# Layer norm, its projection, the second norm and the router's logits as one stage by halves and token tiles, in a fused block on one Trainium2 core

## The reference

```
y = silu(layernorm(conv(...), ln_g, ln_b))
y = y @ w_out
x = x + g1 * y
h = rmsnorm(x, norm_ffn_g[i]) * (1 + sc2) + sh2
grp_logits = (xt @ w_rg + b_rg)          # 4 groups
exp_logits = (xt @ w_re + b_re)          # 32 experts, top 2 in one group
x = x + g2 * hier_moe(h, ...)            # 32 experts: silu(x@gate) * (x@up) @ down
mod = c_act @ ada_w[i] + ada_b[i]        # gives g1, sc2, sh2, g2 ...
```

## Time and profile before

| | us |
|---|---|
| median of 3 runs (2859.23 to 2864.74) | 2859.59 |
| the profiled execution | 2864.43 |
| its span in the trace | 2862.3 |
| stretch from the start of the layer norm to the first expert matmul | 294.6 to 521.5 |
| busy in the whole span: PE, DVE, ACT, POOL | 2546.8, 1608.8, 953.9, 533.8 |

### The profile page before, as it was taken

How to read it: one execution, slowest core, us unless ns; L and a number is a source line. 1 busy time by engine, 2 the same in 40 slices (tenths; PEclk the granted TensorE clock), 3 DMA queues, 4 the chain that set the end, 5 groups by cost and what they waited for, 6 DMA issues and landing times. The chain is left out here.

```text
span 2862.3 us, 40467 instructions
## 1 busy us (share of the span) xinstructions
PE 2546.8 (89%) x15839; PEld 1397.2 (49%) x15839; DVE 1608.8 (56%) x2909; ACT 953.9 (33%) x1486; POOL 533.8 (19%) x476
## 2 busy tenths in 40 slices
PE   4999594799889998589799979998999999999978
PEld 3566343455445554245334447743554554645533
DVE  5876784322222222576499986543665656646742
ACT  6110503121112222555453225522443524514510
POOL 1011123000000000331341100000330411502413
PEclk8999796899999999799899989999999999999999
DMA  9553868599999998320102200043002002020052
GB/s 238 196 168 127 308 221 320 182 375 379 378 377 346 376 368 317 100 70 18 45 30 93 99 30 1 1 155 125 8 1 96 8 9 88 8 89 8 1 210 84
DMA packets 185104, 433.07 MB, mean 151 GB/s; under 512 B 26417, under 2 KB 35889, under 8 KB 184817
## 3 DMA queue, kind: packets, MB, share of 16 engines
q1 hardware_dynamic: 158112, 365.39, 35.8%
q0 software_dynamic: 10176, 32.78, 3.7%
q10 hardware_dynamic: 16656, 32.66, 3.3%
HBM read 371.85 MB, written 58.93 MB: 151 GB/s over the span
## 5 line engine op out<-in xcount | busy, mean ns | idle before, releaser
L1245 PE MATMUL m_gu<-conv_y,m_xT 128*64 128x256 f32 x1024 | 230.9, 384 | 20.2 <-DMA arena<-in_moe_w_up 17.9
L1323 DVE TENSOR_TENSOR m_hid<-m_sg,m_gu 64x256 f32<-64x256 f32 x96 | 39.6, 413 | 341.6 <-ACT m_sg L1293 341.6
L1247 PE MATMUL m_gu<-arena,m_xT 128*64 128x256 f32 x1024 | 230.9, 384 | 0.0
L2291 POOL TENSOR_TENSOR group_words<-steps,consts 128x1024 f32<-128x1024 f32 x32 | 66.0, 2067 | 684.1 <-PE i_pj L142 668.4
L1247 PEld LDWEIGHTS m_gu<-arena,m_xT 128*64 128x64 f32 x1024 | 141.9, 139 | 73.0 <-issue 15.4
L1267 PE MATMUL m_y_ps<-arena,m_hidT 128*64 128x512 f32 x768 | 175.4, 598 | 0.0
L140 PE MATMUL i_pj<-hT,group_words 128*128 128x512 f16 x384 | 146.5, 382 | 15.3 <-DVE group_words L410 9.4
L1245 PEld LDWEIGHTS m_gu<-conv_y,m_xT 128*64 128x64 f32 x1024 | 141.9, 139 | 36.8 <-issue 25.2
L1293 ACT ACT_TABLE_LOAD x48 | 61.6, 1283 | 286.4 <-issue 273.9
L140 PE MATMUL s_pj<-hT,arena 128*128 128x512 f16 x384 | 148.8, 387 | 0.0
L141 PE MATMUL s_pj<-hT,arena 128*128 128x512 f16 x384 | 148.5, 387 | 0.0
(11 more groups left out here) (519 smaller groups left out, 6386.3 us busy)
## 6 DMA issues: line engine op xcount, KB each, us to landing
arena<-in_moe_w_down SPq DMA_DIRECT2D x32, 2048.0 KB, 21.9
arena<-in_moe_w_up SPq DMA_DIRECT2D x22, 2048.0 KB, 24.9
conv_y<-in_moe_w_gate SPq DMA_DIRECT2D x22, 2048.0 KB, 20.8
hT<-in_moe_w_gate SPq DMA_DIRECT2D x10, 2048.0 KB, 21.6
hT<-in_moe_w_up SPq DMA_DIRECT2D x10, 2048.0 KB, 23.2
conv_y<-in_ada_w SPq DMA_DIRECT2D x8, 2048.0 KB, 8.0
x_tok<-in_ada_w ACTq DMA_DIRECT2D x6, 2048.0 KB, 12.7
slot_out<-m_y ACTq DMA_DIRECT2D x96, 128.0 KB, 6.2
```

The source lines that it names most:

```text
L1245: g = nc.tensor.matmul(gu_ps[i][g_rows, 0:FFN // 2], lhsT=xT[:, c, :], rhs=k.wg[e % WEIGHT_SLOTS][:, c, cols], start=c == 0, stop=c == KC - 1)
L1247: u = nc.tensor.matmul(gu_ps[i][u_rows, 0:FFN // 2], lhsT=xT[:, c, :], rhs=k.wu[e % WEIGHT_SLOTS][:, c, cols], start=c == 0, stop=c == KC - 1)
L1323: nc.vector.tensor_tensor(hid[:, i, :], sg[:, i, :], gu_ps[i][u_rows, 0:FFN // 2], ALU.mult) \
L2291: return k.nc.gpsimd.tensor_tensor(k.y_A[:, t % 2], k.adt[:, t, heads].unsqueeze(2).to_broadcast([P, HPG, P]), k.const("after").unsqueeze( ...
```

## The change

The four stages up to the logits become one, `front_stage`. The layer norm goes by halves: the products of token tiles 0 to 2 take channel chunks as the first half comes, and the second half is normalised beside them. The modulation sums stand ahead of the variance on PE, the eight late pieces behind token tiles 3 to 6 on DVE. Each token tile is then gated, added, squared, rooted, normalised, stored (from ACT's queue instead of SP's), transposed and multiplied for its logits. The norm's scale (1 + sc2) is folded into the router's weights, its shift into the router's bias, so `hT` holds the normed tokens without them. PSUM of the mean is reused as the third accumulator and for the transposes. The loads of expert weights stand at other places of SP's list.

```diff
+def front_stage(k):
...
+        ws = arena_units(k, 4, 2).bitcast(F16).rearrange("p (a c n) -> p a c n", a=2, c=KC)
+        normed = arena_units(k, 3).rearrange("p (t d) -> p t d", t=4)
+        ring = [arena_units(k, n).rearrange("p (c n) -> p c n", c=KC) for n in (2, 1)]
+        sums, gate = sb("sums", [P, 4, HALF]), sb("gate", [P, D])
+        rstd, mean1 = sums[:, 0:2], sums[:, 2]
...
+        acc_of, held = [0, 1, 2, 0, 1, 0, 1, 0], {3: 0, 4: 1, 5: 3, 6: 4, 7: 5}
+        turns_behind = {4: (0, 1), 5: (2, 3), 6: (4,), 7: (5, 6)}
+        pieces_behind = {3: (0,), 4: (1, 2), 5: (3, 4, 5), 6: (6, 7)}
...
         @block.sync
...
+            sp.wait_ge(low, 4)
+            sp.dma_start(ring[0], modulation_source(k, pieces[0])).then_inc(ada_in[0], 16)
+            sp.wait_ge(h_low, 2 * KC)
+            sp.dma_start(ring[1], modulation_source(k, pieces[1])).then_inc(ada_in[1], 16)
+            load_gate(k, sp, 0)
+            for n in range(2, len(pieces)):
+                sp.wait_ge(ada_used, n - 1)
+                sp.dma_start(ring[n % 2], modulation_source(k, pieces[n])).then_inc(ada_in[n % 2], 16)
+            sp.wait_ge(ada_used, len(pieces) - 1)
+            load_up(k, sp, 0)
+            sp.wait_ge(ada_used, len(pieces))
+            load_gate(k, sp, 1)
+            sp.wait_ge(mm_done, TT)
+            load_down(k, sp, 0)
+            sp.wait_ge(k.normed_stored, 16 * TT)
+            sp.wait_ge(turned, 2 * TT)
+            load_up(k, sp, 1)
+            load_down(k, sp, 1)
+            sp.wait_ge(added, TT)
+            load_down(k, sp, 2)
+            sp.wait_ge(stored, 16 * TT)
+            sp.dma_start(k.x_tok[:, :, :], natural).then_inc(k.x_natural, 16)
+            sp.wait_ge(lg_done, 1)
+            load_gate(k, sp, 2)
+            load_up(k, sp, 2)
+            sp.wait_ge(zeroed, 64)
         @block.tensor
...
+            def turn(t):
+                pe.wait_ge(normed_ready, t + 1)
+                if t == 0:
+                    pe.wait_ge(gated_done, 3)
+                for h in range(2):
+                    if t:
+                        pe.wait_ge(t_high, 2 * t + h - 1)
+                        pe.wait_ge(t_low, 2 * t + h - 1)
+                    for c in range(4):
+                        at = (4 * h + c) * P
+                        last = nc.tensor.transpose(turned_ps[:, at:at + P], normed[:, t % 4, at:at + P], k.const("ident"))
+                    last.then_inc(turned, 1)
+            def logits(t):
+                if t == 0:
+                    pe.wait_ge(l_high, 1)
+                    pe.wait_ge(l_low, 1)
+                pe.wait_ge(t_high, 2 * t + 2)
+                pe.wait_ge(t_low, 2 * t + 2)
+                for c in range(KC):
+                    last = product(nc, lg_ps[:, t, :], part(k.hT, c, slice(t * P, (t + 1) * P)), part(lws, c),
+                                   c == 0, c == KC - 1)
+                return last
...
+            for c in range(KC):
+                variance(0, c)
...
+            pe.wait_ge(mean_free, 1)
+            for c in range(KC):
+                pe.wait_ge(high, c + 1)
+                pe.wait_ge(low, c + 1)
+                pe.wait_ge(h_high, c + 1)
+                pe.wait_ge(h_low, c + 1)
+                for t in range(3):
+                    last = products(t, c)
+                    if c == KC - 1:
+                        last.then_inc(mm_done, 1)
+                if c:
+                    variance(1, c - 1)
+            variance(1, KC - 1)
+            for t in range(3, TT):
+                pe.wait_ge(gated_done, held[t] + 1)
+                for c in range(KC):
+                    if t == 4:
+                        pe.wait_ge(h_high, KC + c + 1)
+                        pe.wait_ge(h_low, KC + c + 1)
+                    last = products(t, c)
+                last.then_inc(mm_done, 1)
+                for n in turns_behind.get(t, ()):
+                    turn(n)
+                    if n:
+                        logits(n - 1)
+                for n in pieces_behind.get(t - 1, ()):
+                    late_sums(n)
+            turn(TT - 1)
+            logits(TT - 2)
+            logits(TT - 1).then_inc(lg_done, 1)
         @block.vector
...
+            def gate_rows(t):
+                dve.wait_ge(mm_done, t + 1)
+                if t == 1:
+                    dve.wait_ge(zeroed, 64)
+                elif t >= 2:
+                    dve.wait_ge(added, t - 1)
+                v.tensor_tensor(gated[:, t % 2], acc[acc_of[t]], gate[:, :], ALU.mult).then_inc(gated_done, 1)
+            def row_scale(t):
+                dve.wait_ge(row_std, t + 1)
+                v.reciprocal(ss[:, t:t + 1], ss[:, t:t + 1]).then_inc(row_rstd, 1)
+            def turned_low(t):
+                for h in range(2):
+                    dve.wait_ge(t_high, 2 * t + h + 1)
+                    v.tensor_tensor(tile_hT(1, t, h), turned_of(h), tile_hT(0, t, h), ALU.subtract).then_inc(t_low, 1)
+            def piece(n):
+                dve.wait_ge(ada_in[n % 2], 16 * (n // 2 + 1))
+                if n >= 4:
+                    dve.wait_ge(late_mm, n - 3)
+                modulation_products(k, step, ring[n % 2], sums[:, n % 4, :], pieces[n]).then_inc(ada_used, 1)
...
+            gate_rows(0)
+            variance(1)
+            gate_rows(1)
+            invert(1)
+            gate_rows(2)
+            scale(1, 0)
+            for c in range(KC):
+                if c + 1 < KC:
+                    scale(1, c + 1)
+                hidden_low(1, c)
+            for t in range(3):
+                row_scale(t)
...
+            for t in range(3, TT):
+                gate_rows(t)
+                if t == TT - 1:
+                    turned_low(5)
+                row_scale(t)
+                for n in turns_behind.get(t, ()) if t < TT - 1 else (6, 7):
+                    turned_low(n)
+                for n in pieces_behind.get(t, ()):
+                    piece(n)
+            dve.wait_ge(late_mm, len(pieces))
+            dve.wait_ge(lg_done, 1)
...
         @block.scalar
...
+            def row_root(t):
+                slot = normed[:, t % 4, :]
+                act.wait_ge(added, t + 1)
+                if t == 0:
+                    act.wait_ge(low, KC)
+                    act.wait_ge(small_sb, 1)
+                if t >= 4:
+                    act.wait_ge(k.normed_stored, 16 * t)
+                    act.wait_ge(turned, 2 * (t - 3))
+                nc.scalar.activation(slot, k.x_tok[:, t, :], ACT.Square, accum_out=ss[:, t:t + 1]).then_inc(row_squared, 1)
+                act.wait_ge(row_squared, t + 1)
+                nc.scalar.activation(ss[:, t:t + 1], ss[:, t:t + 1], ACT.Sqrt, bias=eps[:, :], scale=1.0 / D) \
+                    .then_inc(row_std, 1)
+            def normalise(t):
+                act.wait_ge(row_rstd, t + 1)
+                nc.scalar.activation(normed[:, t % 4, :], k.x_tok[:, t, :], ACT.Copy, scale=ss[:, t:t + 1]) \
+                    .then_inc(normed_ready, 1)
+                act.wait_ge(normed_ready, t + 1)
+                act.dma_start(k.normed_dram[t * P:(t + 1) * P, :], normed[:, t % 4, :]).then_inc(k.normed_stored, 16)
+            def turned_high(t):
+                for h in range(2):
+                    act.wait_ge(turned, 2 * t + h + 1)
+                    nc.scalar.copy(tile_hT(0, t, h), turned_of(h)).then_inc(t_high, 1)
...
+            square(1, KC - 1)
+            root(1)
+            for t in range(2):
+                row_root(t)
+            for c in range(KC):
+                hidden(1, c)
+            row_root(2)
+            for t in range(3):
+                normalise(t)
+            act.wait_ge(folded, 1)
+            high_part(nc, lws[:, 0], wl[:, :, :]).then_inc(l_high, 1)
+            for t in range(3, TT):
+                if t == TT - 1:
+                    turned_high(5)
+                row_root(t)
+                normalise(t)
+                for n in turns_behind.get(t, ()) if t < TT - 1 else (6, 7):
+                    turned_high(n)
...
 def router_stage(k):
...
-        @block.sync
-        def _(sp):
-            sp.wait_ge(k.normed_stored, 16 * TT)
-            for e in range(2):
-                load_gate(k, sp, e)
-            sp.wait_ge(lg_done, 1)
-            load_gate(k, sp, 2)
-            load_up(k, sp, 2)
...
-            pe.wait_ge(split, 2)
-            for t in range(TT):
-                for c in range(KC):
-                    last = product(nc, lg_ps[:, t, 0:NL], part(k.hT, c, slice(t * P, (t + 1) * P)),
-                                   part(ws, c), c == 0, c == KC - 1)
-            last.then_inc(lg_done, 1)
...
 def mixer_program(nc, ins, out):
...
-                k.next_w_in = k.sem("conv_out_w_in")
-                conv_norm_stage(k)
-            token_projection_stage(k, "co", k.hT, k.mod[:, 2 * KC:3 * KC], pieces=THIRD_PIECES,
-                                   x_to=k.first_dram.rearrange("(p t) d -> p t d", t=TT))
```

(57 more changed lines are left out.)

342 lines of the change are left out of this document (101 added, 241 removed).

## The result

| | before | after |
|---|---|---|
| median, us | 2862.16 (4 runs) | 2888.90 (2886.08 to 2892.83, 4 runs) |
| profiled execution, us | 2864.43 | 2886.08 |
| its span, us | 2862.3 | 2884.3 |
| its mean granted clock | 0.948 | 0.948 |
| first matmul of the first expert, us from the start | 521.52 | 545.86 |

The changed kernel is slower: ratio 1.0095, 95% interval 1.0083 to 1.0107, so 24 to 31 us. One of the four executions behind the median before took 5935.41 us and is left out of the ratio; the other three are those of the table before the change, median 2859.59. The forecast was 2877.6, from 2856 to 2889, with 0.70 on slower. The two profiled executions differ by less, 21.7 us. Up to the first expert the change costs 545.86 - 521.52 = 24.3 us; the experts' stage gives some 2 us back.

What follows compares the result with a forecast made beforehand. It took DVE's loop, then SP held issuing the last weight loads, to bound the stretch before the experts: +20.7 us at the router's start, -2.7 at the gather, so 2859.6 + 18.0 = 2877.6 us, range 2856 to 2889.

Steps and rivals of the forecast that it cites:

- Rival A: End of front stage: SP leaves as it has issued, at about 488, or nobody waits for it; 2858.6 us, chance 0.24.
- the hold: End of front stage: SP's last two weight loads keep it until 505 to 511, taken as 507.5, while all other engines idle.
- Behind 488.6 this gains 2.6 us: End of the loop over tiles 3 to 7: last logits at about 486 against 488.6 before, 2.6 us sooner.
- +20.7: Start of the router's chain: 509.8 instead of 489.1, as SP returns late, so 20.7 us later.
- 20: Loop over tiles 3 to 7: DVE's five waits from gating to root, 4.3 us each, the last partly hidden; 20 us.
- 11.7: Same loop: DVE waits behind each root for ACT's normalisation, store issue and copy, plus second-tile transposes; 11.7 us over five tiles.
- the 22.8 us stall: PE ahead of the transposes of tile 1, with products 5 queued behind: forecast to idle some 22 us.
- 507.5 - 487 = 20.5 us: End of front stage: from the eighth normed store's landing, 486 to 487, to SP's return at 507.5.
- a cold clock in the transposes: PE's transposes in the loop: a lower granted clock may eat a part of the 2.6 us gained at the logits.
- The gather: First gather after the router: 7.0 us becomes about 4.3, the queue being empty by then; -2.7 us.
- Nothing later moves: From the first expert on: weights of experts 0 to 2 land by 526, before about 540, so no further change.
- Rival B: Loop over tiles 3 to 7: late pieces cost 7.9 us each or PE's products run slower; 2892 us, chance 0.08.

## Why the prediction was wrong in size, with its mechanism right

- **Direction, mechanism and place were right.** The router's stage starts late because SP is held in the last two issues. Rival A (SP not held) is refuted by the row; that the hold itself costs the time is shown by the experiments with moved loads, and by the kernel before, where it can be made.
- **The step that failed is "Behind 488.6 this gains 2.6 us"**, and with it the term "+20.7" for the chain's start, which was built on it. The logits came 491.04 - 488.59 = 2.4 us later than before instead of sooner, and the chain's start measured 515.49 - 489.08 = 26.4: 5.7 too low. Of that 5.4 are there before the hold begins: the eighth store landed at 492.4, not at 487. The rest is the stage's end with memsets and scan, 2.5 us for 2.3.
- **Where the 5 us come from.** The first product was 2.2 us late, most of it in the sums and the variance, 7.30 and 8.53 us where I had 6.6 and 7.3. The clock granted there was 0.73 and 0.83, and I had taken the rates from rows at 0.80 and 0.95. The second half ended at 382.4 where I had 378.1, of which 2.1 us are two scalings that took 3.44 us, beside GpSimd's 2.72 us addition. The loop took 109.1 us from there to the end of the logits' instruction where I had 107.3. Of that sum the waits "20" and "11.7" measured 18.6 and 13.1, which cancels. Not in it was the wait of 1.66 us for PE's product of tile 5, which is queued behind the 22.8 us stall; my sum had priced the stall at nothing.
- **The hold, "507.5 - 487 = 20.5 us", measured 512.97 - 492.44 = 20.5, and that is luck.** The transfers behind the eighth store took 533.9 - 492.4 = 41.4 us where I had 39, and SP returned 20.9 us ahead of the last landing where I had taken 526 - 507.5 = 18.5. The two errors of 2.4 us cancel.
- **Without the hold** the router's chain starts at 496.83, against 490.8 under rival A and 489.08 before, and the first expert is 8.3 us late. The early part had five tiles at 384.1 and not at 380, so 14.5 us ahead of 398.6 where I had 19, and the loop gave it all back, as said; a bit more, as it turned out. No run takes the fused stage apart from its loop, so what the halves of the layer norm alone are worth isn't shown.
- **The clock in the front** was not priced; named was only a cold clock in the transposes. The front differs by up to 5 us with it (table), and the changed kernel's profiled execution had the quickest clock of the nine.
- **The gather** took 4.6 us for 4.3 forecast. **"Nothing later moves"** was off by 24.3 - 22.0 = 2.3 us in our favour; I did not look for the cause.
- **The rest of the miss** is not in the trace: 21.7 us between profiled executions, some 27 by the ratio. The profiled execution before stands 2 to 5 us above its kernel's median, the one after 2.8 below.
- **Rival B** (pieces at 7.9 us) did not happen: the pieces took 5.9, seven of their eight instructions 5.48 for 5.47 before. VectorE met GpSimd's addition in the second half instead. The Trainium skill (SBUF — State Buffer, section SBUF: two separate sides) has a VectorE instruction with two inputs in SBUF and a GpSimd one that reads SBUF shut each other out; the trace agrees, 3.44 us for two that take 0.68 each elsewhere, and 2.72 for an addition that takes 2.34 elsewhere.

## What to carry to other kernels

The end of a stage waits for every engine, also for one that only issues transfers: put loads that nobody needs yet at the head of the next stage, and read the duration of an issue as a cost of that engine. Fusing stages moves an engine's idle time into a chain from tile to tile; look in that chain for waits of one engine in which work that now stands behind them would fit, and do the same for every engine's order, since the next one (here PE's stall ahead of the transposes) can become the bound at once. An edit that is slower as a whole may still be worth having: three of its parts put in another place turned 27 us slower into 16.5 us faster.

## What the runs showed of the hardware that I had not expected

- The issue of a 2 MB load took 0.37 to 0.6 us where little was outstanding on its queue, and 3.8 to 10.4 where it was the last of a row of them (both kernels). SP was let go 15 to 21 us ahead of the landing of the load that it was issuing.
- The room is a queue's own: with four of the fourteen megabytes on ACT's queue, SP was let go 29.4 us ahead of the last landing. But the other queue's loads made three of SP's issues longer, 11.8 us against 5.7.
- The clock granted to PE from 298 to 320 us was between 0.64 and 0.81 in the profiled executions of nine kernels whose code for PE is equal there. Each has one such execution, so whether it changes between executions of one kernel isn't shown. The 48 sums took 10.24 us at 0.64 and 7.30 at 0.81, and the stage's first part 67.8 and 62.7.
